# One core's hybrid decoder trunk: a planner's row-queue bounds, the place of a few early stages, the load order, and a line for the samples' last stages

## What is computed

```python
x = x + mixer(rmsnorm(x, norm1))      # projection, mLSTM heads and pooling, output projection
xn = rmsnorm(x, norm2)
q = (xn @ wq).reshape(tokens, 8, 2, 128)
s = einsum('thcd,chkd->thck', q, keys)            # 128 keys a half
...                                               # top 16 of each half, then top 16 of the pairs
ue, ve = u_tab[eidx], v_tab[eidx]                 # 8 heads x 16 experts for each token
act = gelu(einsum('td,thkd->thk', xn, ue))
x = x + einsum('thk,thkd->td', softmax(top) * act, ve)
x = x + sigmoid(x @ w_gate) * (p @ w_ple)
```

## Time and profile before

| | us |
|---|---|
| median of 3 runs (lowest, highest) | 1766.37 (1765.01, 1769.4) |
| time of the profiled execution | 1755.1 |
| its span, first to last instruction | 1753.0 |

### The profile page before, as it was taken

One profiled execution on the slowest core, in us unless ns is written; L12 is line 12 of the kernel. 1 busy time (PEld: TensorE's weight loads), 2 busy tenths in 40 slices (PEclk: granted clock), 3 DMA queues, 4 the chain that ended last, 5 costly groups with the idle time before them and its releaser, 6 DMA issues. The chain is left out here.

```text
span 1753.0 us, 19301 instructions
## 1 busy us (share of the span) xinstructions
PE 1352.5 (77%) x6310; PEld 496.6 (28%) x6310; DVE 997.0 (57%) x2540; ACT 689.7 (39%) x1963; POOL 501.0 (29%) x532
## 2 busy tenths in 40 slices
PE   7888987887668888667677997798666857676766
PEld 4443433343113343211112443343311211111113
DVE  1277668568744355964445434848964434455544
ACT  3146444333435353243333635443443433333334
POOL 0022223222332022243333212222343233333330
PEclk9988988999769999986658898999876875677669
DMA  8599999999999999989999999999999989999993
GB/s 320 192 381 374 409 395 423 386 389 370 381 427 427 378 422 399 388 364 427 427 426 426 426 375 419 418 414 411 368 393 427 427 356 427 427 428 427 427 427 158
DMA packets 96737, 687.26 MB, mean 392 GB/s; under 512 B 11104, under 2 KB 12640, under 8 KB 14318
## 3 DMA queue, kind: packets, MB, share of 16 engines
q0 software_dynamic: 76032, 553.68, 76.4%
q1 hardware_dynamic: 20606, 132.36, 18.7%
HBM read 679.87 MB, written 6.59 MB: 392 GB/s over the span
## 5 line engine op out<-in xcount | busy, mean ns | idle before, releaser
L2125 DVE SCALAR_TENSOR_TENSOR rows<-rows,shown 128x1024 f32<-128x1024 f32 x528 | 638.8, 1221 | 600.5 <-DMA rows<-in_uv,index_B 325.2
L1259 PE MATMUL acc<-rows,weighted 128*64 128x512 f32 x2048 | 695.7, 784 | 232.5 <-ACT weighted L1650 222.7
L1456 POOL DMA_INDIRECT rows<-in_uv,index_A x256 | 243.1, 950 | 683.3 <-PE acc L1259 537.2
L946 PE MATMUL bank<-wring,turned 128*128 128x512 f32 (+1 forms) x840 | 385.9, 607 | 18.3 <-DMA wring<-in_w 18.0
L1456 POOL DMA_INDIRECT rows<-in_uv,index_B x256 | 242.7, 948 | 501.6 <-PE acc L1259 482.4
L1259 PEld LDWEIGHTS acc<-rows,weighted 128*64 128x64 f32 x2048 | 134.7, 161 | 710.7 <-ACT weighted L1650 585.1
L946 PEld LDWEIGHTS bank<-wring,turned 128*128 128x128 f32 x840 | 158.2, 196 | 201.9 <-issue 178.4
L1639 ACT ACTIVATE dots_B<-dots_B 128x1 f32<-128x1 f32 x256 | 51.7, 202 | 361.6 <-DVE rows L2125 359.3
L1639 ACT ACTIVATE dots_A<-dots_A 128x1 f32<-128x1 f32 x256 | 51.2, 200 | 327.4 <-DVE rows L2125 317.7
L1650 ACT ACTIVATE weighted<-consts,dots_A 128x64 f32<-128x64 f32 x256 | 89.0, 348 | 8.4
L1650 ACT ACTIVATE weighted<-consts,dots_B 128x64 f32<-128x64 f32 x256 | 89.0, 348 | 8.4
(11 more groups left out here) (312 smaller groups left out, 986.9 us busy)
## 6 DMA issues: line engine op xcount, KB each, us to landing
wring<-in_w SPq DMA_DIRECT2D x107, 1024.0 KB
out_sample<-scratch SPq DMA_DIRECT2D x2, 2128.5 KB
scratch<-in_c_s SPq DMA_DIRECT2D x2, 2064.0 KB
rows<-in_uv,index_A POOLq DMA_INDIRECT x256
rows<-in_uv,index_B POOLq DMA_INDIRECT x256
keys<-in_keys SPq DMA_DIRECT2D x2, 1024.0 KB
gain<-in_gain SPq DMA_DIRECT2D x3, 640.0 KB
consts<-in_consts SPq DMA_DIRECT2D x1, 1243.0 KB, 10.9
```

What stands on the lines that cost most here:

```text
L946: ins = pe.matmul(ps[:, part], turned["A"][:, 4 * h + c, :], w[:, c, part], start=first, stop=end, skip_group_check=True)
L1259: ins = pe.matmul(acc[c * 64:(c + 1) * 64, :], weighted[:, n % STATS, :], row[:, c * BLOCK:(c + 1) * BLOCK], start=first, stop=end, skip_g ...
L1456: pool.indirect_dma_start(out=rows[:, n % RING, :], out_offset=None, in_=a["uv"], in_offset=bass.IndirectOffsetOnAxis(ap=index[kind][:, pa ...
L2125: dve.scalar_tensor_tensor(u, u, 1.0, shown[:, :, :], ALU.mult, ALU.mult, accum_out=dots[kind][:, part, i:i + 1]).then_inc(u_used, 1)
```

## The change

The change edits the host-side planner and SP's load order. No arithmetic, tile shape, ring size or transfer size changes.

- In pass 0, `show` of the first half tile leaves the dots line and is put behind the first `turn_index`. `("query", 0, 1, 1, 0)` moves from ahead of the first `rank` to behind the first `turn_prob`, and so into a later line.
- `gates`, `project` and `query` no longer need `norm` to start in the plan. Their scale is waited for at their later steps instead (`scale_of`). The order of norms is kept for `turn`, `turn2`, `final` and the samples' `norm`.
- `RUNWAY` is 12.0 for PE and 15.0 for ACT and DVE, where it was 7.0 for all. A row that comes to a nearly empty planned queue takes `SPARSE` (2.75) and not `ROW` (2.47). Some stage costs rise by a few per cent.
- In the last part, the stages of the last tile (5, the samples) other than `embed` become a line of their own beside that of tile 4.
- The loads of layer 0 are spread: gains and pooling weights behind `project` (1, 1), keys behind `project` (2, 1), x of tiles 1 and 2 behind `project` (4, 0). In layer 1 only their order changes.

```diff
     if p == 0:
         early = [("query", 0, FIRST, h, big) for h in range(2)]
-        early += [("turn_pq", big, FIRST), ("match", big, FIRST)] + [("query", 0, 1, h, big) for h in range(2)]
-        out = [e for e in out if e not in early]
+        early += [("turn_pq", big, FIRST), ("match", big, FIRST), ("query", 0, 1, 0, big)]
+        after = [("show", big, 0), ("query", 0, 1, 1, big)]
+        out = [e for e in out if e not in early + after]
         at = out.index(("rank", big, 0, 2))
         out[at:at] = early
+        at = out.index(("turn_index", big, 0, 1)) + 1
+        out[at:at] = after[:1]
+        at = out.index(("turn_prob", big, 0, 1)) + 1
+        out[at:at] = after[1:]
...
-        if g[2] == 0:
+        if g[2] == 0 and g[:2] != PARTS_IN_ORDER[0]:
             out.append(("show", *g[:2]))
...
-    "project": (("PE", 3.4), ("ACT", 0.7)), ...
+    "project": (("PE", 3.55), ("ACT", 0.7)), ...
...
-    "norm": ("turn", "turn2", "final"), "gates": ("turn", "norm"), "forget": ("gates",), "project": ("turn", "norm"), ...
+    "norm": ("turn", "turn2", "final"), "gates": ("turn",), "forget": ("gates",), "project": ("turn",), ...
...
-    "query": ("turn2", "norm"), ...
+    "query": ("turn2",), ...
...
+THIN, SPARSE = 2.0, 2.75
...
-AHEAD, RUNWAY = 8, 7.0
+AHEAD, RUNWAY = 8, {"PE": 12.0, "ACT": 15.0, "DVE": 15.0}
...
+        if stage == "norm" and KIND[t] == "S":
+            found.append(norms[norms.index(e) - 1])
...
-            self.dma = max(self.dma, self.pool + FLIGHT) + ROW
+            self.dma = max(self.dma, self.pool + FLIGHT) + (ROW if self.dma > self.pool + FLIGHT + THIN else SPARSE)
...
+        if stage == "final":
+            waits.append(self.scale_of(e))
...
+    def scale_of(self, e):
+        t = tile_of(e)
+        if e[0] in ("project", "gates"):
+            return self.finish_of(("norm", t, "turn"))
+        if e[0] == "query":
+            return self.finish_of(("norm", t, "turn2"))
+        if e[0] in ("turn", "turn2", "final") and KIND[t] != "S":
+            n = self.norms.index(("norm", t, e[0]))
+            return self.finish_of(self.norms[n - 1]) if n else 0.0
+        return 0.0
...
+            scaled = self.scale_of(e)
+            if scaled is None:
+                return None
+            at = max(at, scaled + SIGNAL)
...
-                dry = self.dma - self.at[engine] < RUNWAY
+                dry = self.dma - self.at[engine] < RUNWAY[engine]
...
+    last = [e for e in closing if e[0] != "embed" and tile_of(e) == PASS_TILES[LAST][-1]]
+    closing = [e for e in closing if e not in last]
     for part in (others, third, fourth, closing):
         lines.append(Line([e for e in part if e not in silent], tuple(lines[1:])))
+    lines.append(Line(last, lines[-1].after))
...
-                    sp.dma_start(keys[:, :, :].rearrange("p a b -> p (a b)"), a["keys"][layer]).then_inc(layer_in, 16)
-                    sp.dma_start(gain2[:, :], a["gain"][layer]).then_inc(layer_in, 16)
-                    sp.dma_start(w_pool[:, :, :].rearrange("p g n -> p (g n)"), a["w_pool"][layer]).then_inc(layer_in, 16)
-                    if layer == 0:
-                        load_tiles()
+                    if layer:
+                        load_pool(layer)
+                        load_keys(layer)
+                if e == ("project", 0, 1, 1, 0):
+                    load_pool(0)
+                if e == ("project", 0, 2, 1, 0):
+                    load_keys(0)
+                if e == ("project", 0, 4, 0, 0):
+                    load_tiles()
```

More of the change, by code:

```diff
@@ L299 @@
     "norm": (("DVE", 0.4),), "gates": (("PE", 1.8), ("DVE", 0.3), ("ACT", 1.2)), "forget": (("DVE", 0.2),),
-    "project": (("PE", 3.4), ("ACT", 0.7)), "cum": (("PE", 0.4), ("DVE", 1.1)), "spread": (("PE", 0.9), ("DVE", 1.7)),
+    "project": (("PE", 3.55), ("ACT", 0.7)), "cum": (("PE", 0.4), ("DVE", 1.1)), "spread": (("PE", 0.9), ("DVE", 1.7)),
     "weigh": (("ACT", 1.6), ("DVE", 0.3), ("ACT", 0.4)), "turn_qk": (("PE", 1.4), ("ACT", 1.3)),
@@ L304 @@
     "scale_heads": (("DVE", 0.9),), "weigh_keys": (("DVE", 0.8),), "pool_r": (("PE", 1.6), ("ACT", 0.7)), "pool": (("PE", 1.0), ("DVE", 0.7)),
-    "heads": (("PE", 0.8), ("DVE", 0.7)), "state": (("PE", 1.2), ("DVE", 1.3)), "mix": (("PE", 3.4), ("DVE", 0.8)),
-    "turn2": (("PE", 1.4), ("DVE", 1.4), ("ACT", 1.0)), "query": (("PE", 3.4), ("ACT", 0.7)),
+    "heads": (("PE", 0.8), ("DVE", 0.7)), "state": (("PE", 1.2), ("DVE", 1.3)), "mix": (("PE", 3.55), ("DVE", 0.8)),
+    "turn2": (("PE", 1.4), ("DVE", 1.4), ("ACT", 1.0)), "query": (("PE", 3.55), ("ACT", 0.7)),
     "turn_pq": (("PE", 0.6), ("ACT", 0.7)), "match": (("PE", 1.0), ("ACT", 0.7)), "rank": (("DVE", 5.0),),
@@ L309 @@
     "turn_index": (("PE", 0.5), ("DVE", 0.3)), "turn_prob": (("PE", 0.5), ("DVE", 0.3)),
-    "turn3": (("PE", 1.4), ("ACT", 1.2)), "gate": (("PE", 3.4), ("ACT", 0.8)), "embed": (("PE", 4.5), ("DVE", 3.4)),
-    "final": (("ACT", 1.7),), "apply": (("DVE", 1.4),), "show": (("PE", 1.8),), "dots": (("DVE", 1.25), ("ACT", 0.9)),
+    "turn3": (("PE", 1.4), ("ACT", 1.2)), "gate": (("PE", 3.55), ("ACT", 0.8)), "embed": (("PE", 4.5), ("DVE", 3.4)),
+    "final": (("ACT", 1.7),), "apply": (("DVE", 1.4),), "show": (("PE", 1.8),), "dots": (("DVE", 1.29), ("ACT", 0.95)),
     "vals": (("PE", 1.1),), "place": (("ACT", 0.7), ("PE", 1.8), ("DVE", 1.3))}
@@ L332 @@
     "sample_args": ("project", "forget"), "sample_read": ("sample_args",), "sample_write": ("sample_read",), "mix": ("heads", "pool"), "turn2": ("mix",),
-    "query": ("turn2", "norm"), "turn_pq": ("query",), "match": ("turn_pq",), "rank": ("match",), "sources": ("rank",), "lists": ("rank",), "pairs": ("lists", "sources"),
+    "query": ("turn2",), "turn_pq": ("query",), "match": ("turn_pq",), "rank": ("match",), "sources": ("rank",), "lists": ("rank",), "pairs": ("lists", "sources"),
     "best": ("pairs",), "soften": ("best",), "choose": ("soften",), "turn_index": ("best",), "turn_prob": ("choose",), "turn_s": ("choose",), "dots": ("show",), "show": ("norm", "dots"),
@@ L417, in needs_of @@
     last, out = {}, {}
+    norms = [e for e in order if e[0] == "norm"]
     for e in order:
@@ L455, in __init__ @@
         self.begun = {}
+        self.norms = [e for e in stage_order if e[0] == "norm"]
         self.cold, self.table = 0.0, None
@@ L1352, in load_tiles, with load_pool, load_keys @@
                 sp.dma_start(x["S"][:, :], a["x_s"]).then_inc(x_rest_in, 16)
+            def load_pool(layer):
+                sp.dma_start(gain2[:, :], a["gain"][layer]).then_inc(layer_in, 16)
+                sp.dma_start(w_pool[:, :, :].rearrange("p g n -> p (g n)"), a["w_pool"][layer]).then_inc(layer_in, 16)
+            def load_keys(layer):
+                sp.dma_start(keys[:, :, :].rearrange("p a b -> p (a b)"), a["keys"][layer]).then_inc(layer_in, 16)
             def load_half(e):
```

12 lines of the change are left out of this document (6 added, 6 removed).

## The result

| | before | after |
|---|---|---|
| median of 4 runs (lowest, highest), us | 1767.01 (1765.01, 1769.4) | 1694.54 (1691.16, 1697.97) |
| ratio, 95% interval | | 0.9589 (0.9566 to 0.9612) |
| time of the profiled execution, us | 1755.1 | 1694.1 |
| its span, us | 1753.0 | 1692.0 |

The account below looks back on a forecast made before the run. Bound by how early the row stream starts, how rarely it runs dry and what follows its last row. Start 10.8, middle 17 and end 4.3 sum to 32 us: 1723 profiled, 1734 scaled to the median; range 1712 to 1760.

Parts of the forecast that it names:

- the gain of the middle: Between first gather and last landing, deeper queues leave the DMA idle less: 17 us, bounds -10 to 35.
- The 4.6 us for the spread loads: At the start, the fourth weight half lands earlier, saving PE's 2.85 us wait and 1.76 us of slow matmuls.
- The 5.9 and 2.8 us for `show` and `query` (1, 1): At the start, the first query begins before `show` (5.9 us), and `turn_index` follows `chosen` at once (2.8 us).
- 8 for DVE, 3.5 for PE and 6 for the small gaps: Middle: three quarters of DVE's dips (8 us), half of PE's (3.5), a quarter of the many small gaps (6).
- five large dips: Middle, idle DMA: two dips with DVE busy, 10.5 us; two with PE busy, 7.0; one before `embed`, 6.2.
- The `embed` wait: At 1410 to 1430 PE stood 10.53 us before `embed`, 6.2 us of idle DMA; it stays, gain 0.
- The margin of 72.3 us: Tile 1's indices are ready at 440.85 and first used at 513.18, so the ranking has time to give.
- Rival 4: Pass 1 starves: dense work is put off until tile 0's rows are used up; 53 us, 1804; chance 0.05.
- Rival 3: Nothing measurable: weight halves are late among deeper rows, 12 us lost in place of 17 won; 1763; chance 0.07.
- Rival 2: The middle is nearly emptied of gaps, 38 us there and 54 in all; 1712; chance 0.09.
- Rivals 1 and 5: 1: only start and end pay, 1751, chance 0.17. 5: another stage takes the start's freed place, 26 us, within forecast's 0.62.
- The end: After the last row, `turned_s` goes ahead of tile 4's `final` on ACT, so the samples' gates begin 4.3 us earlier.

Follow-up runs that it names:

- e7: The changed kernel with both start edits undone (layer's loads all at the start, old places of `show` and `query` (1, 1)): 1699.91 us, ratio 0.9649.
- e11: The changed kernel with only the moves of `show` and `query` (1, 1) undone, spread loads kept: 1693.85 us, ratio 0.9624.
- e4: The kernel before, unchanged, built and profiled once more: 1763.44 us, ratio 1.0004.
- e5: The changed kernel with RUNWAY back at 7 for PE alone, DVE and ACT kept at 15: 1736.76 us, ratio 0.9857.
- e6: The changed kernel with RUNWAY back at 7 for DVE and ACT, PE kept at 12: 1712.63 us, ratio 0.9725.
- e1: The changed kernel with RUNWAY back at 7 for PE, ACT and DVE: 1758.79 us, ratio 0.9947.
- e8: The changed kernel with a buffer of its own for the last `emb`, loaded a pass earlier: 1689.07 us, ratio 0.9585.
- e14: The changed kernel with RUNWAY 20 for PE alone, ACT and DVE kept at 15: 1744.60 us, ratio 0.9898.
- e9: The changed kernel with tile 5's stages back in tile 4's line: 1700.08 us, ratio 0.9668.
- e15: The changed kernel with the last `emb` in its own buffer, the `show` and `query` moves undone and the old needs of `norm`: 1705.12 us, ratio 0.9677.
- e10: The changed kernel with the layer's loads all at the start again, each engine's order kept: 1699.95 us, ratio 0.9660.
- e2: The changed kernel with the plan's old stage costs and SPARSE at 2.47: 1692.58 us, ratio 0.9594.
- e3: The changed kernel with the plan's old needs: gates, project and query begin only after `norm`: 1692.01 us, ratio 0.9593.

## Why the prediction was wrong

In short: the term that failed is the gain of the middle, 17 us, which measured 42.4. Within it, the small gaps and the dips with PE full were put far too low. The terms of the start and of the end came out near their sizes, in part for other reasons than the ones given.

**The start: right at the first gather, wrong in what it is worth.** The first gather is 13.6 us earlier, forecast 13.3. The 4.6 us for the spread loads measure 5.2 there (e7 against e11) and 5.4 to 6.1 in the medians. The Trainium skill, "DMA: Bandwidth & Descriptors", section "Rules for kernel authors", says to issue a transfer early, compute, and wait late. This case agrees for the transfer that is waited for, and not for loads put ahead of it: those held it back, 3.44 us of wait in e7. The 5.9 and 2.8 us for `show` and `query` (1, 1) are 8.7 in the forecast. Undone alone they cost 5.5 at the first gather (e11), since the relaxed needs, costed at nothing, bring some 3 of them by themselves, and they are worth nothing at the end. The forecast named this failure (early first gather, late first `index_B`) but didn't price it. Its "about one half fewer has been fetched, 2.46 us" was right (25.6 MB up to the first gather of before, 24.6 of after). What it lacked is a term for the later first use of `index_B`: 5.4 us of rate that after loses and e11 doesn't.

**The middle: the failed step.** 17 us were forecast, 42.4 came between two profiled executions (47.9 against e4). Its terms, 8 for DVE, 3.5 for PE and 6 for the small gaps, add up to 17.5. Three things were off.

- The size of what could be won. "A share of 0.98 against 1.01 is some 48 us of idle DMA" understates it. By the rate the same stretch lost 77.5. In a thin stretch the DMA engines count as busy while they move less: at 740 to 750 of before the share reads 0.73 with 306 GB/s, at 600 to 610 it reads 0.85 with 307, as 0.72 of 427. This alone did not sink the forecast, for 42.4 would have fitted into 48. What it took of them was too little.
- The split of the dips. I named five large dips and gave PE's kind 7.0 us. Over all stretches of 5 us, those with PE full lost 38.4, those with DVE full 18.3 and both 13.3. By rate the five dips held some 34 us, 11 of them PE's. The many small gaps, 24 us of which I took a quarter, held the other 44, some 28 of it with PE full. From before to after 14.6 went with PE full and 16.0 with DVE full, and 9.9 with both. Taken out of the finished kernel, PE's bound, costed at 3.5, measures 42.2 (e5), and that of DVE with ACT's, costed at 8, 18.1 (e6). The two ways of counting differ by the cost of the next point, which the classes don't split.
- The parts don't add up from before. With a bound of 7 the rest of the change makes the middle 22.5 us longer than it was (17.1 against e4), a cost that I put at nothing, and the deeper bound wins that back too: 65.0 from e1's middle to after's.

The argument for staying "near the middle" of the bounds was also weak: the upper end, 35, was worked out from the share, so the range inherited the error.

**The `embed` wait** stays, as forecast. It is worth 5.5 us by e8's median and 6.9 by its middle, and the forecast had counted 6.2 us of idle DMA there.

**The margin of 72.3 us** was rightly called time that the ranking has to give, and the change uses all of it. **Rival 4**, the starvation of pass 1, didn't happen here but is real. In e14 PE's bound of 20 makes POOL wait 72.6 us for `index_B`, and the time is 50.1 us above after, where the rival's price was 53. That the two are close is luck, for the price was of one such starvation and there were two, with waits of 41.5 and 31.1 us. The place is as described (dense work put off until tile 0's rows are used up). That it takes rows winning nearly every tie was wrong: five or eight more microseconds of bound do it, and it happens twice, before tile 1's and tile 4's rows.

**Rival 3** (halves late among deeper rows) falls. PE's waits for `wring` are 13.6 us, 18.0 before. **Rival 2** was nearest with 1712, for a reason that it gave (gaps nearly emptied); it was low by the same low count of what could be won: 38 for the middle, where 42.4 came. **Rivals 1 and 5** fall with e1 and the timeline.

**The end: right in size, with two errors that cancel.** 4.9 us in the stretches of before and after, 3.7 in those of e9 and after, 5.5 in their medians, forecast 4.3. The idle time fell by the 4.35 us forecast, and the gates' 96 matmuls also ran faster, in 2.83 us where e9 took 4.08 and before 4.70. But "nothing new stands in the way" was wrong. In after ACT still has tile 4's root at 1683.80 and then loads a table until 1685.39, while the samples' gates were done at 1683.94; in e9 that load fell into the time in which ACT waited for PE.

**The scale.** The forecast took the profiled execution as 11.3 us off the median and scaled, as if the profile were always so much quicker. It isn't: after's, e1's and e4's lie within 1 us of their medians. Before's executions spread over 18 us, and the profiled one was among the quickest. So 11 of the 72.5 us are this difference, which no term held.

**Open.** Why the rest of the change lengthens the middle by 22.5 us at a bound of 7 was not taken apart: before with only the deeper bound was not run. A reshuffled plan could do it by chance, as in e15. After was built and timed in one group only, so the terms of 5 us would need it beside e8, e9 and e10 on one chip. Whether a fuller queue makes the executions spread less is open: of the groups of four, before's spread over 4 us, after's over 7 and e8's over 1.5.

## What to carry to other kernels

When a stream bounds a kernel, count what is lost by its rate against the best rate of the same trace, over all short stretches, and class them by the engine that is full. Here the five dips that were looked at held 34 of 77.5 us. Then undo one bound at a time, for the classes alone don't name the cause. A bound that decides how much finished input must be queued before other work may go first had its best value here between two failures (64 us too shallow, 50 us too deep), and the margin to watch is how long the next stage's inputs are ready before their first use: 72.3 us before, 13 in e2 and 3 in e3, which are as fast as after, and none in after, where POOL waits 10.4 us. At zero it has gone far enough. An earlier start is only worth what the next bound lets through; look at the first use of the next tile's indices, not at the first transfer.

## What the runs showed of the hardware that was not expected

- The busy share of the DMA engines is not a measure of their rate. In before's middle it reads 0.98 of 1.01 (3% idle) at 407 of 427 GB/s (5% less).
- A small load among rows takes long from its issue until it is used: after's `emb` is issued at 1347.45 and `embed` starts at 1361.43, 14.0 us later; before it took 13.7. PE stood idle for 10.80 and 10.53 us of these.
- An idle TensorE costs more than the idle time. Before it stood 5.34 us and then did the 96 matmuls of the samples' gates in 4.70, with a mean granted clock of 0.60 in that stretch. After the same idle time they took 4.08 in e9 (0.66), and 5.35 in e4, where the clock was 0.50 all the way, the lower level of 1.2 GHz. In after it stood 0.99 us and did them in 2.83 at a clock of 1.00, the level of 2.4 GHz. The DMA share differs too, and was not varied by itself:

```profile
1741.18:1746.00 4.82, 4.82 (x108) 4.82 (x112) 1.25 (x1) 1.08 (x1) 0.00 (x0) 0.60 0.28 112
```

```profile
1680.25:1683.10 2.85, 2.85 (x105) 2.85 (x109) 0.95 (x2) 1.75 (x3) 0.00 (x0) 1.00 0.03 6
```
